# A second group of Strassen products in each FFN, taken in turns with the last up pieces, every weight split of that stretch on VectorE

## What is computed

```
def swiglu(x, w_gate, w_up, w_down):
    return (jax.nn.silu(x @ w_gate) * (x @ w_up)) @ w_down
x = x + 0.5 * swiglu(rmsnorm(x, ffn1_norm[l]), ffn1_w_gate[l], ffn1_w_up[l], ffn1_w_down[l])
```

## Time and profile before

| | before |
|---|---|
| median of 3 runs | 1335.14 us (1334.80 to 1335.16) |
| the profiled execution | 1334.76 us, of which the span of instructions 1333.0 us |
| TensorE busy | 1324.6 us, 99% of the span, 7312 matmuls |
| VectorE, ScalarE, GpSimd busy | 62%, 59%, 37% |
| mean granted TensorE clock | 0.999 of full speed |
| moved by DMA | 256.91 MB, 193 GB/s on average |

### The profile page before, as it was taken

How to read it: one execution, slowest core, us unless ns; L and a number is a source line. 1 busy time by engine, 2 the same in 40 slices (tenths; PEclk the granted TensorE clock), 3 DMA queues, 4 the chain that set the end, 5 groups by cost and what they waited for, 6 DMA issues and landing times.

```text
span 1333.0 us, 18862 instructions
## 1 busy us (share of the span) xinstructions
PE 1324.6 (99%) x7312; PEld 1119.5 (84%) x7312; DVE 822.4 (62%) x1066; ACT 789.8 (59%) x1083; POOL 494.1 (37%) x204
## 2 busy tenths in 40 slices
PE   9999999999999999999999999999999999999998
PEld 8888888888888888888888877788888888888887
DVE  6657856945556875557856659754335642555776
ACT  7655467456555566555557697577434655655553
POOL 1463023474547104463023321035525524445500
PEclk9999999999999999999999999999999999999999
DMA  9656864234655785555865655355854443655483
GB/s 347 224 188 211 240 240 156 96 121 151 217 187 185 178 303 194 189 189 156 247 234 178 229 179 196 112 178 175 296 175 176 175 172 128 205 186 182 169 228 119
DMA packets 41114, 256.91 MB, mean 193 GB/s; under 512 B 6192, under 2 KB 6736, under 8 KB 12112
## 3 DMA queue, kind: packets, MB, share of 16 engines
q1 hardware_dynamic: 36832, 230.89, 49.6%
q0 software_dynamic: 2304, 16.78, 6.8%
q10 hardware_dynamic: 1904, 8.23, 1.7%
HBM read 254.80 MB, written 1.08 MB: 192 GB/s over the span
## 4 chain that ended last, share of the span: by engine, by line
PE 95%; DVE 2%; ACT 2%; issue 1%; DMA 0%; POOLq 0%; POOL 0%; ACTq 0%; SPq 0%; DVEq 0%
PE acc L376 20%; PE acc L361 14%; PE acc L363 14%; PE acc L362 14%; PE acc L377 12%; PE acc L379 3%; PE acc L2820 2%; PE work L1171 1%; PE acc L2821 1%; PE acc L618 1%; PE acc L619 1%; PE acc L617 1%; PE work L618 1%; PE work L617 1%; PE work L619 1%; PE work L1256 1%
## 5 line engine op out<-in xcount | busy, mean ns | idle before, releaser
L342 POOL TENSOR_TENSOR wlo<-raw,whi 128x2048 fp32r<-128x2048 f32 x80 | 381.9, 4774 | 492.7 <-ACT whi L337 485.1
L337 ACT ACTIVATE whi<-raw 128x2048 fp32r<-128x2048 f32 (+1 forms) x237 | 438.8, 1858 | 100.1 <-PE acc L363 45.6
L342 DVE TENSOR_TENSOR wlo<-raw,whi 128x2048 fp32r<-128x2048 f32 (+1 forms) x157 | 359.7, 2295 | 172.1 <-ACT whi L337 171.7
L376 PE MATMUL acc<-xT,whi 128*128 128x512 f32 x1208 | 428.0, 396 | 0.2
L377 PE MATMUL acc<-xT,wlo 128*128 128x256 f32 x1384 | 373.6, 280 | 0.0
L376 PEld LDWEIGHTS acc<-xT,whi 128*128 128x128 f32 x1208 | 226.5, 188 | 51.8 <-DVE work L839 1.8
L377 PEld LDWEIGHTS acc<-xT,wlo 128*128 128x128 f32 x1384 | 261.2, 189 | 7.0
L361 PE MATMUL acc<-whi,xT 128*128 128x512 f32 x416 | 168.4, 405 | 0.0
L363 PE MATMUL acc<-whi,xT 128*128 128x512 f32 x416 | 162.5, 391 | 0.0
L362 PE MATMUL acc<-wlo,xT 128*128 128x512 f32 x416 | 162.3, 390 | 0.0
L839 DVE TENSOR_TENSOR work<-acc,low_parts 128x512 f32<-128x512 f32 x88 | 61.5, 698 | 84.6 <-ACT low_parts L721 82.6
(11 more groups left out here) (436 smaller groups left out, 1923.1 us busy)
## 6 DMA issues: line engine op xcount, KB each, us to landing
raw<-in_t_ffn_up SPq DMA_DIRECT2D x85, 1024.0 KB, 5.0
raw<-in_t_m_in SPq DMA_DIRECT2D x52, 1024.0 KB, 4.9
raw<-in_t_ffn_down SPq DMA_DIRECT2D x32, 1024.0 KB, 5.5
raw<-in_t_ffn_down POOLq DMA_DIRECT2D x16, 1024.0 KB, 8.4
raw<-in_t_ffn_down SPq DMA_DIRECT2D x16, 512.0 KB, 6.6
raw<-in_t_m_os SPq DMA_DIRECT2D x8, 1024.0 KB, 5.0
raw<-in_t_m_out SPq DMA_DIRECT2D x4, 1024.0 KB, 4.9
sum_rows<-row_scratch ACTq DMA_DIRECT2D x4, 1024.0 KB, 4.6
```

What stands on the lines that cost most here:

```text
L337: act.activation(granule(whi, u, i), granule(raw, u, i), ACT.Copy).then_inc(hi_ready, 1)
L342: eng.tensor_tensor(granule(wlo, u, i), granule(raw, u, i), granule(whi, u, i).bitcast(F32), ALU.subtract).then_inc(lo_signal(g)[0], 1)
L376: pe.matmul(to, hi[:, c], both_parts(kt), start=first, stop=False)
```

## The change

The up pieces and the entries of the down part become one list of 40 "places" per FFN, one block of the ring each. Places 0 to 9 are the up pieces 0 to 9. From place 10 the table is

The core of the difference:

```diff
-        hidden_needed = {0: 8, 1: 12, 3: 16, 5: 20, 7: 22}
-        for n, (kts, half, product) in enumerate(DOWN):
+        for n, entry in LATE.items():
+            u, i = place(f, n)
+            if entry[0] == "up":
+                up(entry[1])
+            elif entry[0] == "product":
+                _, group, name = entry
+                k = product_index(group, name)
+                if name == "P4":
+                    pe.wait_ge(hidlo_done, PIECES * f + KD * (group + 1))
+                if name == "P6":
+                    pe.wait_ge(forms_split, 2 * (2 * f + group + 1))
+                if k >= 2:
+                    pe.wait_ge(products_added, products_so_far(f, group, name) - 2)
+                multiply_form(pe, u, group, name)
+                if n == LAST_UNIT - 1 and b + 1 != B_OUT:
+                    transpose_x(pe, b + 1, 0)
...
+        hi(8)
+        for n in range(5, LAST_UNIT):
+            entry = LATE.get(n, ("up", n))
+            if entry[0] == "up":
+                low(entry[1])
+                hi(n + 4)
+                silu(entry[1])
+                round_hidden(entry[1])
+            elif n < LAST_UNIT - 1:
+                hi(n + 4)
+            if n == 9:
+                round_forms(0)
+            if n == 23:
+                act.wait_ge(gran_done, place_done(f, n))
+                round_forms(1)
...
+            if n in (10, 24):
+                rest_forms((10, 24).index(n))
+            if entry[0] == "up":
+                m = entry[1]
+                join(m)
+                row(m)
+                lo(n + 3)
+                product(m)
+                rest_hidden(m)
+            elif entry[0] == "product":
+                if n < 35:
+                    lo(n + 3)
+                if n == 35:
+                    lo(38)
+                    lo(39)
...
+                add_product(n, *entry[1:])
...
+        def make_forms(group):
+            pool.wait_ge(hidlo_done, PIECES * f + KD * (group + 1))
...
+        lo(9)
...
+        make_forms(0)
+        add_to_slot(15)
+        add_to_slot(17)
+        add_to_slot(19)
+        add_to_slot(23)
+        make_forms(1)
+        add_to_slot(29)
+        add_to_slot(31)
+        add_to_slot(33)
+        add_to_slot(37)
```

More of the change, by code:

```diff
@@ L89, in add_ffn @@
         add(f"ffn{f}.up0")
-        for c in range(1, NCH):
+        for c in range(1, LATE_FROM // 2):
             add(f"ffn{f}.up{c}", [tuple(range(KD))] * 2)
-        for j in range(len(DOWN) // 2):
-            add(f"ffn{f}.down{j}", [kts for kts, _, _ in DOWN[2 * j:2 * j + 2]])
+        for n in range(LATE_FROM, LAST_UNIT):
+            add(f"ffn{f}.place{n}", [rows_of(LATE[n])])
+        add(f"ffn{f}.last", [rows_of(LATE[n]) for n in range(LAST_UNIT, PLACES)])
     add_ffn(0)
@@ L578, in ffn_loads @@
             up(1)
[L579 to L585, removed]
-        for n, (kts, half, product) in enumerate(DOWN):
-            if n not in ADDED_TO_SLOT:
-                load(sp, units[f"ffn{f}.down{n // 2}"], n % 2, down_tiles[half])
+        for c in range(2, LATE_FROM // 2):
+            up(c)
+        for n, entry in LATE.items():
+            if entry[0] == "up":
+                c, i = divmod(entry[1], 2)
+                load(sp, *place(f, n), up_tiles[c][:, i * SLOT:(i + 1) * SLOT])
+            elif entry[0] == "block":
+                load(sp, *place(f, n), down_tiles[entry[1]])
+            elif entry[2] not in ADDED_TO_SLOT:
+                load(sp, *place(f, n), down_tiles[BLOCK_OF_W[entry[2]][1]])
+            if f == 0 and n == place_of_piece(21):
+                for dst, param in PARAMS:
+                    sp.dma_start(dst, param).then_inc(params_loaded, 16)
     ROW_OF = (0, 1, 2, 4)
@@ L604, in build, with product_index @@
[L604 to L619, removed]
+    def product_index(group, name):
+        return len(PRODUCTS) * group + PRODUCTS.index(name)
@@ new lines, in product_bank, with products_so_far, multiply_form @@
+    def product_bank(group, name):
+        return work[:, 2 + product_index(group, name) % 2, :]
+    def products_so_far(f, group, name):
+        return 2 * len(PRODUCTS) * f + product_index(group, name) + 1
+    BACK_OF_X = pair(0)
+    def multiply_form(pe, u, group, name):
+        wait_lo(pe, u.g)
+        hi, lo = granule(whi, u, 0), granule(wlo, u, 0)
+        i, j, summed = TOKENS_OF[name]
+        tok, first = slice(i * P, (i + 1) * P), KD * group + 4 * j
+        bank = product_bank(group, name)
+        for k in range(4):
+            ahi = form_hi[:, 4 * j + k, tok] if summed else hid_hi[:, first + k, tok]
+            alo = form_lo[j][:, k, tok] if summed else hid_lo[:, first + k, tok]
+            pe.matmul(bank, ahi, hi[:, k, :], start=k == 0, stop=False)
+            pe.matmul(bank, ahi, lo[:, k, :], start=False, stop=False)
+            mm = pe.matmul(bank, alo, hi[:, k, :], start=False, stop=k == 3)
```

373 lines of the change are left out of this document (150 added, 223 removed).

## The result

The changed kernel takes 1376.31 us, median of 4 runs (1375.95 to 1378.80), against 1335.04 before: 1.0313 times the time, 95% interval 1.0296 to 1.0331, so 41 us slower. The forecast was 1371, slower, in a range of 1344 to 1394.

A forecast was written before the change was run, and what follows sets the result against it. TensorE, busy 99% of the span, was taken as the bound. Waits of 4 x (3.5 + 7.3) + 3 x 1.5 = 47.7 us, less 11.7 of saved work, gave +36.0: 1371 us, range 1344 to 1394.

The forecast's parts named there:

- TensorE's own work: Twelve matmuls fewer per FFN, 10.9 us in four FFNs, and four loop exits, 0.8: -11.7 us.
- VectorE's pace: Late stretch: VectorE needs 8.0 us per product and piece, TensorE 8.27; it keeps up, regaining about 0.25 per pair.
- VectorE's busy share in the late stretches: Sign expected in the changed kernel's profile: above 90%.
- Group 0: First sums of hidden blocks: weights split at 27.7 us after piece 7, needed at 24.9; TensorE waits 2.8 us.
- Group 1: Second sums: weights split at 31.4 us after place 20, TensorE has 24.8; it waits 6.6 us.
- the lateness brought along: VectorE 2.6 us late at piece 12, three pairs give back about 1.2, leaving 1.4 at piece 15.
- The mutual lock: VectorE's splits and GpSimd's sums exclude each other; two splits lengthen each group's sums from 10.3 to 14.7 us.
- the rival's own sum: Rival, chance 0.09: sums made in 10.3 us, VectorE not late, TensorE waits for nothing; 1323 us.
- The neighbours: Place behind each P6 wait: TensorE waits 0.7 us more, in both groups of each FFN.
- The turn: Before the transposes to the next stage: TensorE waits 1.5 us in three FFNs, bounds 0 and 3.3.
- The clock: Rival, chance 0.12: clock falls to 1.2 GHz after long waits, adding 11 us (1382) or 22 (1393).
- Transfers late: Rival, chance 0.12: slower adding transfers cost TensorE about 1 us at each of seven, 7 per FFN; 1399 us.

The follow-up runs named there:

- better_tail: Kernel better with VectorE's split for place 39 moved behind the finished first half of x: 1331.42 us, ratio 0.9976 against the kernel before.
- reorder_late: Changed kernel with products reordered so sums are needed one pair later, and ScalarE's rounding and VectorE's rests two places later: 1417.17 us, ratio 1.0617.
- no_sums: Changed kernel without GpSimd's sums of group 1 and the four small ones of group 0: 1332.64 us, ratio 0.9982.
- better: Changed kernel with products reordered, wide sums started early, rounding and rests re-placed, adding transfers issued between small sums: 1336.02 us, ratio 1.0013.
- plain_dma: Changed kernel with the eight adding transfers of each FFN copying in place of adding: 1371.20 us, ratio 1.0273.

## Why the prediction was right, point by point

- **TensorE's own work, -11.7.** Held in the count, 48 matmuls, and less in the time: without sums the kernel is 2.1 us faster than before with 5 us of new waits and 1.6 of slow matmuls left in it, so about 9 of the 11.7 reach the time. The working took a piece at 5.55 us; that is the shorter of two values (5.56 and 5.64), and between products the longer one holds.
- **VectorE's pace, 8.0 of 8.27 per pair.** VectorE's part held: in FFN 2 the join of one piece starts at 608.20 and that of the next at 616.20. TensorE's pair is 5.64 + 2.72 = 8.36, so VectorE regains 0.36 per pair and not 0.25, and it never made TensorE wait by its pace alone. What was not in the forecast is that with so little slack one late block (FFN 2) is carried into the next chain. One sign did not come: VectorE's busy share in the late stretches was to be above 90%, and from the end of piece 9 to the end of piece 21 it is 81 to 83%, since VectorE itself stands idle for the rounded sums, 6.68 us in FFN 2 (row 665.42 above).
- **Group 0, 27.7 us from the end of piece 7, so a wait of 2.8.** In FFN 2 the join of piece 7 starts at 576.91, which puts its end near 576.1; P6 starts at 603.69, 27.6 later. The sums took 14.3 for the 14.7 forecast. The wait came out at 2.3, since TensorE itself took some 0.3 longer than 24.9.
- **Group 1, 31.4 us, so 6.6.** Right in size in FFN 2 (gap 7.1), too large in the other three (4.8 to 5.4). The sums with the split ahead of them were put at 16.9 and took 16.4, alike in all FFNs; TensorE's three pairs took 25.1 for 24.8. What was oversized most is the lateness brought along, 1.4 us: over its usual 0.83 from TensorE's end, the join of piece 15 is 0.2, 0.8, 2.5 and 0.4 late in FFN 0 to 3. At piece 12 VectorE was 2.6 late as forecast in FFN 1, but three pairs gave back 1.8 there and not 1.2 (the forecast's own pair times add up to 1.4, and TensorE's pairs are longer). That the forecast fits FFN 2 is luck, since there it is the late block that makes VectorE late. The spread among the FFNs is in when the sums start, not in how long they last.
- **The mutual lock.** The step on which the verdict hung. Without it the sums would have been covered, by the rival's own sum, and 10.3 us became 14.3 and 16.4. In the trace of the change a wide sum lasts 2.40 us where no split runs beside it and 4.34 to 4.5 beside one, a small one 1.29 and 3.2 to 3.3: each split met costs the sums some 2 us, two splits in group 0 and three in group 1. Either engine can be the one that pays: in FFN 2 a single wide sum of better_tail took 4.39 where two took 4.88 before, beside a split that kept its 2.28; in FFN 0 of the change a split of VectorE took 4.45 beside the second wide sum (first row: the split of better_tail; second: that of the change):

```profile
617.67 2.28 DVE L373 TENSOR_TENSOR wlo<-raw,whi 128x2048 fp32r<-128x2048 f32 x1
126.00 4.45 DVE L373 TENSOR_TENSOR wlo<-raw,whi 128x2048 fp32r<-128x2048 f32 x1
```

  The sum alone is 2.44, and in better_tail it began 0.17 behind a split of 2.28, which so had 2.11 left: 2.44 + 2.11 = 4.55, 0.16 from the 4.39. The rule of the Trainium skill ("SBUF — State Buffer", section "Who interferes with whom") that the forecast named, exclusion for a whole instruction, agrees with these rows.
- **The neighbours, 0.7 each, 5.6.** Mis-sized: only 1.2. The block behind P6 was late by 0.6 where P6 ran at full speed (FFN 1 and 2, group 0); where P6 ran at the lower clock it took 1.7 longer, which covered it.
- **The turn, 1.5 three times.** Right on average (2.7, 1.7, 0.6), within the bounds of 0 and 3.3, and different each time, which the working had no term for.
- **The clock.** The step that failed. The sum left it out and the rival had it at 0.12, as something instead of the forecast. It is part of it: 12.7 us, beside the rival's 11. A fall costs less than the rival had it (2.7 for a whole product, about 1.5 to 2.6 measured), and the falls at products were six, between its cases of four and eight. The forecast lands 5 us from the result by luck: its waits were 8 us too long, and stood in for most of what the clock cost.
- **Transfers late, 0.12.** A small part is true: plain copies give 5 us, from one late block in FFN 2 and one turn, not from each of seven transfers. And "the adding transfer stands behind the sums and costs nothing" was right in the change, at 15 us before its use, but reorder_late shows how little it takes to lose that.

The causes are told apart: sums away takes the waits at the products, and the clock's falls with them, less work for VectorE hardly does, and the order of products alone does nothing. Left open is why a wait of 2.13 us is followed by the lower clock and one of 2.23 is not.

## What to carry to other kernels

Count the matmuls saved last: here they were 11 us of TensorE's work, and the order that saved them cut the room of a chain through GpSimd, ScalarE and VectorE from 75 us to 25, into which two engines that shut each other out did not fit. Price a wait that you add for TensorE with what its clock loses behind it, and look at what stands behind the waiting instruction on its engine: neither moving a step later nor giving it more places helps if the queue in front of it (here a rounding that waits for a transfer) is late by the same cause. What did help was starting each part of the chain as soon as its own inputs were there, and issuing a transfer in the middle of a chain in place of behind it.

## What the runs showed that I had not expected

- The lower clock came behind waits as short as 2.13 us, in two of four cases, and behind every wait of 4.6 us or more in the change; in no_sums it came with one of 2.5, in better a wait of 3.2 went without it, and in better_tail, with none over 1.8, it never came.
- A fallen clock is not all loss: the matmuls at 0.43 give VectorE time. Group 1's sums started earliest in FFN 0 and 3 (waits 4.6 and 4.8), whose group 0 had lost the clock, and later in FFN 1 and 2 (5.3 and 7.0), which had not. In plain_dma the clock fell at group 0 in FFN 1 alone, and FFN 1 has the shortest wait at group 1, 4.4 beside 5.2 three times.
- One late block costs more where an engine has no slack: of VectorE's 2.68 us of idling in FFN 2 some 1.7 came back at the next wait of TensorE, 45 us later (7.0 in place of the 5.3 of FFN 1).
